# Gating rows from a copy, sample queries as four stationary quadrants, and the first weight slabs issued in turn

## What is computed

```
z = gelu(x @ w_in); u, v = split(z)          # v has 2048 columns
v = layer_norm(v, ln_g, ln_b)                # rows of the last chunk of 128 are an output (sg_v)
mixed = tril(w_s) applied over the 128 tokens of a chunk, per group of 256 columns, + bias
y = (u * mixed) @ w_out
...
S = exp(g) * S + k^T v ;  o = q S            # GLA: one step for each of 16 samples and 4 heads
o = rms_norm(o) * silu(g_out)                # S is 128 x 256 per sample and head, in and out
```

## Time and profile before

| | |
|---|---|
| median of 3 runs | 1682.74 us (1681.32 to 1683.12) |
| the profiled execution | 1676.87 us |
| span of its slowest core (7) | 1675.3 us, of the fastest (2) 1656.4 us |
| PE busy | 1616.8 us, 97% of the span |
| VectorE, ScalarE, POOL busy | 43%, 38%, 15% |
| chain that ended last | PE 89%, DMA 7% |

### The profile page before, as it was taken

One profiled execution on the slowest core, in us unless ns is written; L12 is line 12 of the kernel. 1 busy time (PEld: TensorE's weight loads), 2 busy tenths in 40 slices (PEclk: granted clock), 3 DMA queues, 4 the chain that ended last, 5 costly groups with the idle time before them and its releaser, 6 DMA issues.

```text
span 1675.3 us, 28918 instructions; the slowest of 8 cores (1656.4 to 1675.3 us)
## 1 busy us (share of the span) xinstructions
PE 1616.8 (97%) x10121; PEld 890.1 (53%) x10121; DVE 724.3 (43%) x1362; ACT 640.7 (38%) x1257; POOL 245.1 (15%) x353
## 2 busy tenths in 40 slices
PE   2999999999999999999999899999999999999998
PEld 1457456665456654444444344444445666667643
DVE  2577542223346673111355555333244567622233
ACT  2553441122356672111344335322243677412111
POOL 1232120001112131000112011000012212200000
PEclk8999999999999999999999899999999999999999
DMA  8895275346190186557259873948724505953511
GB/s 173 115 144 76 44 114 76 51 56 84 16 150 1 20 120 105 77 83 119 101 130 152 159 101 62 201 110 155 148 63 74 91 2 78 150 76 55 85 51 53
DMA packets 144338, 155.84 MB, mean 93 GB/s; under 512 B 7410, under 2 KB 137060, under 8 KB 144196
## 3 DMA queue, kind: packets, MB, share of 16 engines
q0 software_dynamic: 116576, 111.47, 46.7%
q1 hardware_dynamic: 27620, 42.53, 8.4%
HBM read 246.89 MB, written 18.55 MB: 158 GB/s over the span
## 4 chain that ended last, share of the span: by engine, by line
PE 89%; DMA 7%; issue 1%; DVE 1%; ACT 1%; POOL 0%; DVEq 0%; POOLq 0%; ACTq 0%; SPq 0%
PE ps L563 87%; DMA t<-sg_w_in 2%; DMA t<-gla_w_in 2%; PE ps L582 2%; DMA sgvp<-t 1%; DMA t<-ffn_w 1%; ACT t L505 1%; DVE t L516 1%; POOL t L539 0%; DVE t L531 0%; DVE t L979 0%; DVE t L792 0%; DVEq L1190 0%; DVEq L1172 0%; DVE t L796 0%
## 5 line engine op out<-in xcount | busy, mean ns | idle before, releaser
L563 PE MATMUL ps<-t,t 128*128 128x512 bf16 (+7 forms) x9353 | 1587.7, 335 | 41.3 <-DMA t<-sg_w_in 20.3
L563 PEld LDWEIGHTS ps<-t,t 128*128 128x128 bf16 (+3 forms) x9353 | 844.9, 99 | 745.1 <-issue 65.8
L505 ACT ACTIVATE t<-ps 128x512 bf16<-128x512 f32 (+5 forms) x719 | 378.8, 537 | 776.4 <-PE ps L563 739.9
L516 DVE TENSOR_TENSOR t<-t,ps 128x512 bf16<-128x512 bf16 (+3 forms) x264 | 131.4, 511 | 425.2 <-PE ps L563 424.1
L516 DVE TENSOR_TENSOR t<-ps,t 128x512 f32<-128x512 f32 (+3 forms) x212 | 176.0, 842 | 273.8 <-PE ps L563 196.9
L539 POOL TENSOR_TENSOR t<-t,t 128x1 f32<-128x1 f32 (+2 forms) x170 | 109.5, 645 | 591.4 <-DVE t L525 294.9
L505 ACT ACTIVATE t<-t 128x1024 bf16<-128x1024 f32 (+3 forms) x153 | 119.3, 781 | 179.1 <-DVE t L531 159.4
L590 POOL DMA_DIRECT2D t<-ffn_w x72 | 63.9, 887 | 571.1 <-PE ps L563 503.7
L505 ACT ACTIVATE t<-t,t 128x1024 bf16<-128x1024 f32 (+2 forms) x76 | 94.7, 1247 | 63.5 <-POOL t L539 59.6
L531 DVE SCALAR_TENSOR_TENSOR t<-t,t,t 128x1024 f32<-128x1024 f32 (+2 forms) x69 | 88.6, 1286 | 41.8 <-POOL t L539 41.4
L531 DVE SCALAR_TENSOR_TENSOR t<-ps,t,t 128x256 bf16<-128x256 f32 (+3 forms) x148 | 79.3, 577 | 30.2 <-PE ps L563 22.7
(11 more groups left out here) (29 smaller groups left out, 130.9 us busy)
## 6 DMA issues: line engine op xcount, KB each, us to landing
t<-ffn_w POOLq DMA_DIRECT2D x56, 1024.0 KB, 12.2
t<-sg_w_in POOLq DMA_DIRECT2D x16, 1024.0 KB, 14.6
t<-gla_w_in POOLq DMA_DIRECT2D x12, 1024.0 KB, 14.4
t<-xp SPq DMA_DIRECT2D x16, 512.0 KB, 5.1
t<-sg_w_out POOLq DMA_DIRECT2D x8, 1024.0 KB, 12.3
t<-st_in SPq DMA_DIRECT2D x64, 128.0 KB, 3.6
sts<-t SPq DMA_DIRECT2D x64, 128.0 KB, 3.7
yp<-t SPq DMA_DIRECT2D x15, 512.0 KB, 2.8
```

Source lines behind the costliest of these rows:

```text
L505: return e.activation(out=rz(out), in_=rz(in_), func=func, scale=scale, **kw)
L516: return P.op(eng, lambda e: e.tensor_tensor(out=rz(out), in0=rz(a), in1=rz(b), op=op), [a, b], [out], cost, prio=prio, after=after)
L563: ins_ = e.matmul(o, rz(l), rz(r), start=a, stop=b)
```

## The change

The order of the first slabs and x tiles: seven x tiles wait for the first slab, where six did, and each of the slabs 1 to 3 gets a wait of its own. The gating rows of the last tile are made from a copy `vcp` of its v, in the two halves of `tmp`, whose halves are now tracked apart (`LV.parts`). The samples' queries become stationary: `Qm` holds, per head and sample, the head's 16 query columns with all but one set to zero, and one group of four matmuls (one head each, in its own quarter of PE's columns) takes the four bf16 states of a sample as moving operands and adds into one PSUM bank over all samples. The sixteen turning matmuls go. The states have five buffers, the bf16 states four. The planner's rate for slabs goes from 0.29 to 0.25 MB per us.

```
-    def __init__(self, bank, n, f32, make):
-        self.bank, self.n, self.f32, self.make = bank, n, f32, make
+    def __init__(self, bank, a, b, f32, make):
+        self.bank, self.a, self.b, self.n, self.f32, self.make = bank, a, b, b - a, f32, make
     def parts(self):
-        return 1
+        return sum(1 << k for k in range(self.a // 64, (self.b - 1) // 64 + 1))
...
                 if e == POOL:
-                    dma_work = max(dma_work, st) + o["nbytes"] / 0.29e6
+                    dma_work = max(dma_work, st) + o["nbytes"] / 0.25e6
                     fin = dma_work + 1.5
...
     EGs = alloc([128, 4, NS], F32, ax, XL)
-    oTs = alloc([128, 8, NS], F32, ax, XL)
+    Qm = alloc([128, 4, NS, NS], BF16, ax, XL)
     Kmask = [alloc([128, 512], BF16, ax, XL) for _ in range(1)]
-    NSS = 6
+    NSS = 5
     Sch = [alloc([128, 256], F32, ax, XL) for _ in range(NSS)]
-    Snb = [alloc([128, 256], BF16, ax, XL) for _ in range(2)]
+    Snb = [alloc([128, 256], BF16, ax, XL) for _ in range(4)]
+    colmask = alloc([128, NS, NS], BF16, [ax[0] - 2048], XL)
+    vcp = alloc([128, 16, 128], BF16, [XL - 4096], XL)
...
     first_slab = slab("sg_w_in", 0, 0, 8, 2048, 512)
-    xl.append(load_x(0, 1))
-    for t in range(2, TPS):
+    for t in range(1, TPS):
         xl.append(load_x(0, t, slab_ops[0:1]))
...
             return v if shape is None else v.rearrange("p (a b) -> p a b", b=shape)
-        return LV(res, b - a, res.kind == "tmp", make)
+        return LV(res, a, b, res.kind == "tmp", make)
...
                 load(lbc[0:np_, :], sg_ln_b[0, qs].partition_broadcast(np_), "c9", 262144, after=slab_ops[-1:])
-                tr_ = Res("tmp")
-                tq = part(tr_, np_, 0, 512)
-                tq_ = part(tr_, np_, 0, 512, None if np_ == NS else 128)
+                if q % 2 == 0:
+                    tr_ = Res("tmp")
+                o_ = q % 2 * 512
+                tq = part(tr_, np_, o_, o_ + 512)
+                tq_ = part(tr_, np_, o_, o_ + 512, None if np_ == NS else 128)
                 ts(tq_, quarters[q], c(10, np_), c(11, np_), ALU.mult, ALU.add)
...
                 tt(tq, tq, lbc[0:np_, :], ALU.add)
-                store(dst[:, qs], tq, "sgv%d" % (q % 2), np_ * 2048)
+                store(dst[:, qs], tq, "sgv%d" % (q % 2), np_ * 2048, slack=2.0)
                 if np_ == NS:
-                    t3 = part(tr_, np_, 0, 512, 256)
+                    t3 = part(tr_, np_, o_, o_ + 512, 256)
                     gs = slice(q * 2, q * 2 + 2)
...
             if s == 0:
-                gate = slab_ops[0:1] if nb == 1 else []
+                gate = [[], powers[4:5], powers[8:9] + slab_ops[1:2], slab_ops[2:3]][nb]
             else:
...
                     last = s == NSB - 1 and t == TPS - 1
+                    if last:
+                        copy(vcp[:], v[:, :, colsof(t)])
                     layer_norm(128, t, v[:, :, colsof(t)],
-                               (sgvp, [v[:, q * 4:(q + 1) * 4, colsof(t)] for q in range(4)]) if last else None)
+                               (sgvp, [vcp[:, q * 4:(q + 1) * 4, :] for q in range(4)]) if last else None)
             if s == 0 and nb == 1:
...
         c = newstat()
+        def head_of(h):
+            if ob.kind == "tmp":
+                return part(ob, np_, h * 256, (h + 1) * 256)
+            return PV(ob, np_, 256, h * 256)
         for h in range(4):
-            act(small("junk", np_, 0, 256), PV(ob, np_, 256, h * 256), AF.Square, scale=1.0 / 16, accum=c(h, np_))
+            act(small("junk", np_, 0, 256), head_of(h), AF.Square, scale=1.0 / 16, accum=c(h, np_))
         ts(c(4, np_, 4), c(0, np_, 4), EPS, None, ALU.add)
...
         for h in range(4):
-            stt(og_(h * 256, (h + 1) * 256), PV(ob, np_, 256, h * 256), c(8 + h, np_),
+            stt(og_(h * 256, (h + 1) * 256), head_of(h), c(8 + h, np_),
                 sg[0:np_, h * 256:(h + 1) * 256], ALU.mult, ALU.mult)
...
         memset(Kmask[0][:], 0.0)
+        P.op(POOL, lambda e: e.memset(colmask[:], 0.0), [], [colmask[:]], 0.3)
+        P.op(POOL, lambda e: e.affine_select(out=colmask[:], in_=colmask[:], pattern=[[1, 16], [-1, 16]],
+                                             compare_op=ALU.not_equal, fill=1.0, base=0, channel_multiplier=0),
+             [colmask[:]], [colmask[:]], 0.5)
+        for h in range(4):
+            tt(Qm[:, h, :, :], qS[:, h, :].unsqueeze(1).to_broadcast([128, NS, NS]), colmask[:], ALU.mult)
         b = Res("ps")
...
         got = {}
-        for k in range(-5, total + 1):
-            if k + 5 < total:
-                got[k + 5] = load(Sch[(k + 5) % NSS][:], st_in[(k + 5) // 4, (k + 5) % 4], "si%d" % ((k + 5) % NSS), 131072, slack=4.0)
+        for k in range(-4, total + 1):
+            if k + 4 < total:
+                got[k + 4] = load(Sch[(k + 4) % NSS][:], st_in[(k + 4) // 4, (k + 4) % 4], "si%d" % ((k + 4) % NSS),
+                                  131072, slack=4.0)
             if 0 <= k < total:
...
                 stt(S_[:], S_[:], EGs[:, h, j:j + 1], PV(sb, 128, 256), ALU.mult, ALU.add)
-                act(Snb[k % 2][:], S_[:], AF.Copy)
+                act(Snb[h][:], S_[:], AF.Copy)
                 store(sts[j, h], S_[:], "so%d" % (k % NSS), 131072, slack=2.0)
-            if k >= 1:
-                j, h = (k - 1) // 4, (k - 1) % 4
-                mms([(PV(oT, 128, 1, (2 * h + v) * NS + j), [(Snb[(k - 1) % 2][:, v * 128:(v + 1) * 128],
-                                                            qS[:, h, j:j + 1])], True, True, False) for v in range(2)])
+            if k >= 0 and k % 4 == 3:
+                j = k // 4
+                mms([(PV(oT, NS, 256, 0, p0=32 * h), [(Qm[:, h, j, :], Snb[h][:])], j == 0, j == NS - 1, True)
+                     for h in range(4)], slow=0.3)
             yield k
-        copy(oTs[:].rearrange("p c j -> p (c j)"), PV(oT, 128, 8 * NS))
-        ob = Res("ps", 2)
-        for k in range(2):
-            mms([(PV(ob, NS, 128, c * 128), [(oTs[:, c, :], identf[:, :])], True, True, False)
-                 for c in range(4 * k, 4 * k + 4)], slow=4)
+        tr_ = Res("tmp")
+        for h in range(4):
+            copy(part(tr_, NS, h * 256, (h + 1) * 256), PV(oT, NS, 256, 0, p0=32 * h))
+        ob = tr_
         hr = Res("hb")
```

## The result

The changed kernel takes 1657.74 us (median of 4 runs, 1653.91 to 1658.92) against 1682.03 before: a ratio of 0.9853, 95% interval 0.9833 to 0.9874, 24.3 us less. The prediction was 1662, range 1650 to 1673.

The account below looks back on a forecast made before the run. Time was taken as PE's work plus idle stretches plus half-clock work. Core 7's terms, 14 + 9 + 0 + 1.5 = 24.5, and core 3's 17.9 gave a middle of 21: 1682.74 - 21 = 1662 us, range 1650 to 1673.

Parts of the forecast that it names:

- The first slabs: Kernel start: slab 1 lands sooner, PE reaches it without a wait, u columns start at 87.2 not 102.2; 14 us gained.
- T: Landing time of slab 0 at the kernel start: 15.8 us before, forecast to fall by 1.7 to 14.0.
- The rival of late slabs: At the start, slabs issued one by one come late, so the start gains 5 in place of 14: 1671; chance 0.13.
- The gating rows: Last tile's gating, core 7: of 9.9 us PE loss, 9 gained, as only the third quarter waits for stores.
- The 3.3 us of the third quarter's wait: Gating rows: VectorE's one remaining store wait, a store of 11.1 us against 7.8 of column blocks between.
- The samples: Sample states: 5.4 us of matmuls removed, 5.4 added by sixteen quartered groups; sum 0.
- the fifth rival: Sample groups: each change of form costs a whole large matmul, 0.216, 32 times: 6.9 more, 1669; chance 0.05.
- The slab rate: Near 465.6 us, where POOL stood in a slab issue and PE idled: planner expecting slabs later gains 1.5 us.
- The sum: Whole kernel on core 7: 14 + 9 + 0 + 1.5 = 24.5 us gained, to a span of 1650.8.
- the middle of 17.9 and 24.5: Whole kernel: 21 us gained, between 17.9 if core 3 is slowest and core 7's 24.5.
- the order there stays: Core 3 at 911 us: it lost 6.2 us as POOL stood in a slab issue; that order was to remain.
- The state buffers: Rival on sample steps: five buffers for six could make every step 0.54 us longer, 35 in all: 1697; chance 0.04.

## Why the prediction was right

**The first slabs** were forecast by the right mechanism and nearly to size. T was 14.77 (14.0 forecast), slab 1 issued 14.3 us after it (13.1) and there after another 12.8 (11.9); slabs 2 and 3 landed before they were needed. PE waited for none of them, and the u columns began 14.3 us earlier on core 7. The term was 14; the new start alone measured 14.6 to 15.5. The rival of late slabs did not decide, though it was near: slabs 1, 2 and 3 landed at 41.9, 54.9 and 71.3 us, 2.9, 1.3 and 3.1 later than assumed, and were needed at 42.4, 58.1 and 72.4, also 1.8 to 3.2 later than assumed. The 11.9 us were not of a slab alone as the prediction has it: slab 2 of the kernel before, issued at 17.2, was in flight until 46.1, and slab 3 had been issued at 41.5.

**The gating rows** are the term that was mis-sized: 9 forecast, 2.7 by the ratio and 3.8 in the mean for this part alone, and about 5 on core 7 of the changed kernel (2.96 idle and 1.7 at half clock left of 9.9). It was sized on core 7, one of the two cores that lost most here (7.8 us of idle, the mean of the eight 4.7); and core 3, which was to have nothing to gain, lost 1.8 behind the row that I had read. Beyond that, two steps of it failed. "The third and fourth quarters' own following work waits for no store" was true, but that work waits for the gain and bias rows, which have one buffer each and land 11 to 14 us after issue; I had read the stores alone, because before the change the rows came while VectorE waited for stores. And the halves, on which the term was built, are worth nothing: the copy, which I had only charged, is what frees PE, as the two kernels with one of them show. The 3.3 us of the third quarter's wait were 7.0: the store had its 11.2, but only some 4 us of other work stood in between instead of 7.8. VectorE, late from waiting for rows, found those column blocks' matmuls done and went through them at its own pace: between 918.5 and 922.7 us it waits for PE once, 0.32 (first row), and then for the store (second row). With two sets of rows the wait for the store is gone as well, on every core, though the planner orders that kernel anew.

```profile
921.62 0.75 DVE L535 SCALAR_TENSOR_TENSOR t<-ps,t,t 128x512 bf16<-128x512 f32 x1 [0.32 <-PE ps L567]
...
929.73 1.00 DVE L529 TENSOR_SCALAR t<-t,t 128x512 f32<-128x512 bf16 x2 [7.03 <-DMA sgvp<-t]
```

**The samples** were right: a group 0.31 (0.34), two single columns 0.054 each step, nothing in sum. The Trainium skill's rule that a change of tiling mode drains TensorE ("TensorEngine Tiling (Array Packing)", Key Properties) agrees with the 0.09 us ahead of a group and the 0.22 to the next matmul, where four matmuls at once would need 0.108; nothing like a whole large matmul for each change, which was the fifth rival.

**The slab rate** was undersized: 1.5 forecast, 3.3 to 5 alone. With the new start it is worth 0 on average, but it keeps waits from the slower cores.

**The sum** came out near by luck: core 7's 22.6 is not made as its 24.5 was. Two windows of the kernel before, and the two of the changed one with the same work in the main:

```profile
440.00:560.00 120.00, 115.15 (x924) 70.26 (x922) 63.55 (x118) 69.75 (x142) 22.28 (x32) 0.99 0.39 58
870.00:970.00 100.00, 91.82 (x494) 43.92 (x493) 58.05 (x120) 42.61 (x63) 15.31 (x21) 0.95 0.87 137
```

```profile
425.00:545.00 120.00, 118.22 (x955) 72.20 (x955) 67.35 (x125) 71.89 (x148) 23.31 (x35) 1.00 0.40 58
850.00:950.00 100.00, 94.50 (x512) 45.89 (x511) 58.60 (x123) 37.38 (x54) 14.98 (x21) 0.97 1.03 147
```

Where the rate's 1.5 was put, PE idles 3.1 us less (4.9 to 1.8), and a stretch at half clock is gone. Around the gating rows, with the wait for POOL ahead of them, it idles 2.7 less (8.2 to 5.5) where 9 were forecast: that wait grew on core 7 from 0.4 us to 2.5. So a term that was too large and one that was too small made up for each other.

**The slowest core.** That a wait for POOL falls on some core or other, and that the middle of 17.9 and 24.5 should be taken, held by luck as much as by reason: core 3, which was to keep its wait, had one of 1.4 us in its place, and core 0 was the slowest. The runs with two sets of rows and with the last u slab behind four powers show the mechanism right. The term "the order there stays" was right, its size on each core was not to be known.

**The state buffers** deserved their small chance: waits for `st_in` appear on four of eight cores, up to 3.0 us, and even four buffers do not change the time.

## What to carry to other kernels

Ask of a wait that is taken away what else the same instructions read: a resource with one buffer that was hidden behind the old wait (here the rows) is next in line. If a producer and an output path share a buffer, a private copy for the output path can be worth more than a second buffer in it, as here. A loss read on the slowest core can be far above the mean (here 7.8 us against 4.7): read the same place on all cores before it goes into a sum. A queue that issues transfers and also computes small values for norms can hold the whole machine up when a transfer is late (here up to 9.6 us at one place): order the small values first.

## What was not expected of the hardware

The cores come in pairs, 0 and 1, 2 and 3, 4 and 5, 6 and 7: when one core of a pair ends early, the other ends late. In the kernel with the gating rows alone the spans are

```profile
core 0: 1656.3 us, clock 0.994
core 1: 1674.7 us, clock 0.988
core 2: 1656.2 us, clock 0.992
core 3: 1679.3 us, clock 0.987
core 4: 1678.9 us, clock 0.990
core 5: 1655.2 us, clock 0.994
core 6: 1665.6 us, clock 0.990
core 7: 1678.8 us, clock 0.987
```

Which of the two it is changes from run to run. Of any two cores one is ahead, so the test is against cores of different pairs: over the 34 runs of the kernel before in the three sets, the two cores of a pair differ by 11.0 us on average, two cores of different pairs by 7.8. The faster core of a pair took 1664.5 us on average in the first set and the slower 1675.5; in the changed kernel 1644.9 and 1653.1. The slower one's slabs land later: with the last u slab behind the powers, core 0 (1641.1 us) and core 1 (1647.5) have these medians over 56 transfers, and in all four pairs of that run the faster core has 11.5 to 12.0 and the slower 12.5 to 12.9.

```profile
t<-ffn_w POOLq DMA_DIRECT2D x56, 1024.0 KB, 12.0
```

```profile
t<-ffn_w POOLq DMA_DIRECT2D x56, 1024.0 KB, 12.9
```

So a wait for a late transfer falls on one core of a pair more than on the other: with two sets of rows the gap near 888 us is 6.0 to 9.6 us on the slower core of each pair and at most 1.8 on the faster, and the time is that of a slower one. What couples the two cores, no run here shows.
